# Small tensors behind the large ones in SBUF, convolved rows on a 64-byte step, and the sum of squares of the first half earlier at one of the layer boundaries

## The reference, cut to what matters

```
def rms_norm(x, g, eps):
    y = x * rsqrt(mean(x * x, axis=-1) + eps)
    return y * g

def causal_dwconv(x, w):          # out[t] = sum_j w[j] * x[t - 2 + j]
    ...

def hybrid_mixer(h, ...):
    proj = h @ w_in               # q, k, v of 2 dilated and 4 differential head pairs, 3 gated-conv groups
    ...                           # rotary, two kinds of attention, gated short convolution
    return concatenate([o_a, o_b, o_c]) @ w_out

def conv_glu_ffn(h, w_up, conv_w, w_down):
    g, u = split(h @ w_up)        # 22 tiles of 128 features
    g = causal_dwconv(g, conv_w)
    return (silu(g) * u) @ w_down

for layer in range(2):
    h = h + hybrid_mixer(rms_norm(h, norm_mix_g[layer]), ...)
    h = h + conv_glu_ffn(rms_norm(h, norm_ffn_g[layer]), ...)
return rms_norm(h, final_g)
```

## Time and profile before

| | |
|---|---|
| median of 3 runs | 2671.3 us |
| the profiled execution's own time | 2670.58 us |
| its span | 2668.6 us |
| mean granted PE clock | 0.969 of full |
| PE busy | 2489.0 us (93%) |
| DVE, POOL, ACT busy | 1525.8, 1189.1, 883.2 us |
| DMA | 130.28 MB, mean 49 GB/s |

### The profile page before, as it was taken

The page is one execution under the profiler, slowest core; times in us unless marked ns, Lnnn a source line. Parts: engine busy times, 40 slices in busy tenths (PEclk is TensorE's granted clock), DMA queues, the critical chain, the costliest instruction groups (busy, mean ns, idle before and its releaser), DMA issues.

```text
span 2668.6 us, 30947 instructions
## 1 busy us (share of the span) xinstructions
PE 2489.0 (93%) x11478; PEld 2014.4 (75%) x11478; DVE 1525.8 (57%) x2177; ACT 883.2 (33%) x1667; POOL 1189.1 (45%) x766
## 2 busy tenths in 40 slices
PE   8799999896999999999979999979879999999996
PEld 6688877774788888888768888768658888788884
DVE  8544677538555555555664456773575555555545
ACT  3344444313323232322414344442233232222322
POOL 3111122246666666665421112131576666566563
PEclk9899999897999999999989999989899999999998
DMA  3000011210111111111310010111101111111111
GB/s 138 24 25 25 31 32 43 80 56 16 48 51 60 48 48 48 64 51 60 109 46 25 24 32 25 32 62 44 48 32 48 48 64 52 59 48 48 48 48 63
DMA packets 53637, 130.28 MB, mean 49 GB/s; under 512 B 4720, under 2 KB 22256, under 8 KB 53488
## 3 DMA queue, kind: packets, MB, share of 16 engines
q1 hardware_dynamic: 51904, 127.03, 14.4%
q10 hardware_dynamic: 1584, 1.28, 0.2%
HBM read 118.59 MB, written 9.44 MB: 48 GB/s over the span
## 4 chain that ended last, share of the span: by engine, by line
PE 77%; DVE 12%; POOL 5%; issue 2%; ACT 2%; DMA 0%; POOLq 0%; DVEq 0%; SPq 0%; ACTq 0%
PE ps L744 16%; PE ps L745 16%; PE ps L746 16%; PE ps L711 6%; PE ps L713 6%; PE ps L712 6%; PE ps L938 3%; PE ps L925 2%; DVE h L1406 2%; POOL w_hi L544 2%; PE ps L912 1%; PE ps L913 1%; ACT prob L1168 1%; POOL w_lo L552 1%; DVE h L1404 1%
## 5 line engine op out<-in xcount | busy, mean ns | idle before, releaser
L518 POOL CAST w_hi<-stage 128x1024 fp32r<-128x1024 f32 (+1 forms) x66 | 67.7, 1026 | 860.1 <-PE ps L713 798.1
L711 PE MATMUL ps<-x_hi,w_hi 128*128 128x512 f32 x960 | 396.4, 413 | 9.1 <-issue 6.0
L552 POOL TENSOR_TENSOR w_lo<-more_stage,w_hi 128x512 fp32r<-128x512 f32 x202 | 289.3, 1432 | 225.1 <-ACT w_hi L1237 209.0
L713 PE MATMUL ps<-x_hi,w_lo 128*128 128x512 f32 x960 | 382.2, 398 | 0.0
L712 PE MATMUL ps<-x_lo,w_hi 128*128 128x512 f32 x960 | 382.0, 398 | 0.0
L552 POOL TENSOR_TENSOR w_lo<-stage,w_hi 128x512 fp32r<-128x512 f32 x194 | 276.8, 1427 | 229.1 <-ACT w_hi L1237 213.9
L1343 DVE TENSOR_TENSOR h<-ps,h 128x1024 f32<-128x1024 f32 x160 | 195.9, 1225 | 199.2 <-PE ps L746 196.2
L744 PE MATMUL ps<-T_hi,w_hi 128*128 128x512 f32 x704 | 285.1, 405 | 24.0 <-POOLq L555 8.8
L744 PE MATMUL ps<-mix,w_hi 128*128 128x512 f32 x704 | 281.3, 400 | 5.5 <-POOLq L555 5.5
L745 PE MATMUL ps<-T_lo,w_hi 128*128 128x512 f32 x704 | 282.1, 401 | 0.0
L746 PE MATMUL ps<-T_hi,w_lo 128*128 128x512 f32 x704 | 282.0, 401 | 0.0
(11 more groups left out here) (197 smaller groups left out, 4593.8 us busy)
## 6 DMA issues: line engine op xcount, KB each, us to landing
stage<-stream SPq DMA_DIRECT2D x112, 512.0 KB, 3.6
more_stage<-stream SPq DMA_DIRECT2D x68, 512.0 KB, 4.3
h<-x_t SPq DMA_DIRECT2D x16, 512.0 KB, 6.3
stage<-stream SPq DMA_DIRECT2D x16, 448.0 KB, 4.5
saved_h<-h SPq DMA_DIRECT2D x8, 512.0 KB, 4.8
h<-saved_h SPq DMA_DIRECT2D x8, 512.0 KB, 3.3
out_t<-h SPq DMA_DIRECT2D x16, 256.0 KB, 2.1
stage<-stream SPq DMA_DIRECT2D x16, 64.0 KB, 4.8
```

Of the source, the lines that this page charges most:

```text
L518: pool.tensor_copy(w_hi[:, s, wide], stage[:, s, wide]).then_inc(pool_seq, 1)
L552: pool.tensor_tensor(block_of(w_lo, n), raw, block_of(w_hi, n).bitcast(f32), ALU.subtract)\
L711: pe.matmul(out, w_hi[:, s, w], hi, start=start, stop=False)
L713: return pe.matmul(out, w_lo[:, s, w], hi, start=False, stop=stop)
```

## The change

Two things are changed.

The first is the layout. `padded`, `eye`, `ones`, `vec`, `gain` and six more small tensors are declared behind `more_stage`, the last of the large ones, with `eye` and `ones` ahead of `padded`. The zeros ahead of the convolved row become 16 (64 bytes) in place of 2; all slices of `padded` that began at TAPS - 1 begin at PAD. Starts in bytes beyond a multiple of 64, from the sizes of the tensors:

| | before | after |
|---|---|---|
| `h`, `stage`, `w_hi`, `w_lo`, `q_next`, `k_next` | 0 | 0 |
| `x_hi`, `x_lo`, `q_split`, `k_twice`, `k_lo`, `mix`, `prob`, `v_next`, `T`/`B` blocks, `more_stage` | 32 | 0 |
| centre of `padded` (read at L1227, used at L938, L1127, L1676) | 8 | 0 |
| `padded` one back, two back (L1704) | 4, 0 | 60, 56 |
| `eye`, `ones`, `vec` | 32 | 0 |

The second is the order of PE in `start_normed` where `fed` is not None, that is once in the program, between the feed-forward of layer 0 and the attention of layer 1.

```diff
+PAD = 16
...
-        padded = sbuf("padded", [P, TAPS - 1 + SEQ])
-        eye, ones = sbuf("eye", [P, P]), sbuf("ones", [P, P])
-        vec = sbuf("vec", [P, DEPTH, NV])
...
         more_stage = sbuf("more_stage", [P, F_SLOTS - W_SLOTS, D_MODEL])
+
+        eye, ones = sbuf("eye", [P, P]), sbuf("ones", [P, P])
+        padded = sbuf("padded", [P, PAD + SEQ])
+        vec = sbuf("vec", [P, DEPTH, NV])
...
                 heads_of_x(0, 1)
+                if fed is not None:
+                    sum_squares(0)
                 rests_of_x(0, 1)
                 heads_of_x(1, 1)
-                sum_squares(0)
+                if fed is not None:
+                    spread(0)
+                else:
+                    sum_squares(0)
                 rests_of_x(1, 1)
                 n = next_tile()
-                project_half(n, 0, THIRD[0], {3: lambda: spread(0), 6: lambda: sum_squares(1)})
+                if fed is not None:
+                    project_half(n, 0, THIRD[0], {6: lambda: sum_squares(1)})
+                else:
+                    project_half(n, 0, THIRD[0], {3: lambda: spread(0), 6: lambda: sum_squares(1)})
...
-                    dve.scalar_tensor_tensor(k_next[:, :], padded[:, TAPS - 1 - back:TAPS - 1 - back + SEQ], tap,
+                    dve.scalar_tensor_tensor(k_next[:, :], padded[:, PAD - back:PAD - back + SEQ], tap,
...
-            dve.memset(padded[:, 0:TAPS - 1], 0.0).then_inc(dve_seq, 1)
+            dve.memset(padded[:, 0:PAD], 0.0).then_inc(dve_seq, 1)
```

More of the change, by code:

```diff
@@ L252, in build @@
         more_stage = sbuf("more_stage", [P, F_SLOTS - W_SLOTS, D_MODEL])
+        eye, ones = sbuf("eye", [P, P]), sbuf("ones", [P, P])
+        padded = sbuf("padded", [P, PAD + SEQ])
+        vec = sbuf("vec", [P, DEPTH, NV])
+        gain = sbuf("gain", [P, KT])
+        neg_top = sbuf("neg_top", [P, 2, 2])
+        total_share = sbuf("total_share", [P, 2, 2, 2])
+        total, share = total_share[:, 0, :, :], total_share[:, 1, :, :]
+        head_sums = sbuf("head_sums", [P, 2, QB])
+        factor = sbuf("factor", [P, 2])
+        rs = sbuf("rs", [P, 3, QB])
         ps = ctx.enter_context(nc.psum_tensor("ps", [P, 8, HALF], f32))
@@ L267, in build @@
         squares = ((q_next[:, :], k_next[:, :], v_next[:, :], v_cur[:, :, :].rearrange("p b d -> p (b d)"),
-                    padded[:, TAPS - 1:], prob[:, 0, 1, :], prob[:, 1, 0, :], prob[:, 1, 1, :]),
+                    padded[:, PAD:], prob[:, 0, 1, :], prob[:, 1, 0, :], prob[:, 1, 1, :]),
                    (q_next[:, :], k_next[:, :], heads[:, :, :].rearrange("p b d -> p (b d)"), rstd_all[:, :],
-                    cos_t[:, :], sin_t[:, :], padded[:, TAPS - 1:]))
+                    cos_t[:, :], sin_t[:, :], padded[:, PAD:]))
         final_heads = v_next[:, :].rearrange("p (b d) -> p b d", d=P)
         diagonal = squares[0][0]
-        turned_groups = (padded[:, TAPS - 1:TAPS - 1 + HALF], padded[:, TAPS - 1 + HALF:])
+        turned_groups = (padded[:, PAD:PAD + HALF], padded[:, PAD + HALF:])
         low, high = slice(0, HEAD_DIM), slice(HEAD_DIM, P)
@@ L1089, in keep_first @@
                 act.wait_ge(product_done, PRODUCTS * (layer * F_TILES + f) + 1)
-                out = q_next[:, 0:HALF] if f else padded[:, TAPS - 1:TAPS - 1 + HALF]
+                out = q_next[:, 0:HALF] if f else padded[:, PAD:PAD + HALF]
                 act.activation(out, bank(STEADY[0][2]), ACT.Copy).then_inc(first_kept, 1)
@@ L1226, in conv_center @@
                 act.wait_ge(gate_ready, seen(gate_ready))
-                act.activation(out, padded[:, TAPS - 1:], ACT.Copy, scale=tap).then_inc(gate_used, 1)
+                act.activation(out, padded[:, PAD:], ACT.Copy, scale=tap).then_inc(gate_used, 1)
             def round_blocks(count):
@@ L1628, in first_blocks @@
                     rest("B21", k)
-                add_product(layer, 0, 2, padded[:, TAPS - 1:TAPS - 1 + HALF], 1, q_next[:, 0:HALF], first_kept)
+                add_product(layer, 0, 2, padded[:, PAD:PAD + HALF], 1, q_next[:, 0:HALF], first_kept)
                 dve.wait_ge(spread_done, 2 * norm + 2)
@@ L1649, in first_blocks @@
                     form("T4", k, "T2", "B21", ALU.subtract)
-                gates = padded[:, TAPS - 1:]
+                gates = padded[:, PAD:]
                 u2 = u3 = gates[:, 0:HALF]
@@ L1679, in combine @@
             def combine(layer, f):
-                gates, ups = padded[:, TAPS - 1:], q_next[:, :]
+                gates, ups = padded[:, PAD:], q_next[:, :]
                 low_gates, high_gates, low_ups, high_ups = gates[:, 0:HALF], gates[:, HALF:], ups[:, 0:HALF], ups[:, HALF:]
```

## The result

The changed kernel takes 2633.08 us (median of 4 runs, 2631.03 to 2633.65) against 2672.45 for the kernel before in the same series (4 runs, 2667.46 to 2674.71): ratio 0.9854, 95% interval 0.9837 to 0.9871. That is 39.4 us faster; 4.8 were predicted and 2655 was the low end of the range. The profiled execution took 2631.03 us, its span is 2629.2. What follows shows that the order gave some 3 to 7 us, about as predicted, and the layout about 35, where the prediction had put 0.

A forecast was written before the change was run, and what follows sets the result against it. PE, busy 93% of the span, was taken as the bound. The order's 3.15 + 1.65 = 4.8 us, with 0 for the layout, took 2671.3 to 2666.5, stated as 2666 us; range 2655 to 2673.

The forecast's parts named there:

- The order's term: Boundary into layer 1: PE's 3.15 us wait ahead of sum_squares(1) goes, with 1.65 us of low clock behind: 4.8 us.
- The steps: Boundary chain: sum_squares(0) without wait, roots(0) sooner, partial(1) ready before PE needs it, first scores 4.8 us sooner.
- One step: Boundary: with one POOL collision counted, DVE has partial(1) ready 2.4 us before PE arrives, so PE doesn't wait.
- Rival 1: Boundary gain doesn't reach the end: POOL and DVE meet otherwise or clock falls elsewhere; 2669 to 2673 us, chance 0.15.
- DVE, ACT and POOL: Layout on these engines: new row starts worth 0, though POOL's final-norm sum with `padded` goes from 1089 to 1290 ns.
- the cover named: Final norm: POOL's last sum ends 3.3 us before DVE asks for it, against 0.4 us of slowing.
- PE's moving side, taken as 0: Three-pass matmuls: moving rows going from 32 to 0 bytes were expected to change the spacing of 233.3 ns by nothing.
- The bounds, 3.3 ns either way: Phase effect per matmul, from wide scores at 230 ns against 233.3: -29 to +29 us over 8,880 matmuls.
- Rival 2: Three-pass matmuls: PE's moving reads get faster when rows start at 64 bytes; 2637 to 2658 us, chance 0.12.
- rival 3: Three-pass matmuls get slower because weights and moving rows now start at equal phases; 2695 us, chance 0.05.
- a nanosecond is worth 8.9 us: Each nanosecond saved on each of about 8,880 three-pass matmuls shortens the kernel by 8.9 us.

The follow-up runs named there:

- e1: The kernel before with only PE's new order at the boundary into layer 1, old layout kept: 2664.99 us, ratio to before 0.9978.
- e7: The changed kernel with 2 zeros instead of 16 ahead of the convolved row, its centre at 8 bytes again: 2630.48 us, ratio to before 0.9843.
- e3: The changed kernel with a 32-byte tensor ahead of everything large, so weights and moving rows all start at 32: 2630.14 us, ratio to before 0.9846.
- e4: The changed kernel with weights `w_hi` and `w_lo` at 32 bytes and moving rows at 0 of 64: 2666.75 us, ratio to before 0.9982.
- e8: The changed kernel with DVE's product of gate and value put behind its first down-projection add in ten pairs per layer: 2620.23 us, ratio to before 0.9803.

## Why the prediction was wrong

- **The order's term was right.** 4.8 us were predicted from two rows. The stretch to the first scores went from 65.2 to 60.4 us in the changed kernel, and by 4.3 us in e1, where no matmul is faster. e1 is the fair test; that the changed kernel shows 4.8 to the digit is in part luck, since the layout bears on that stretch too (65.8 us with the layout alone). The steps held: sum_squares(0) right behind heads(0,1) with no wait, DVE's idle time 2.61 us where 2.9 was said, an add of partial(1) colliding with POOL once more for 2.76 us, a clock of 1.00 behind, and 11.39 us ahead of the scores. One step was off by a little: partial(1)'s last three adds take 4.94 us, where partial(0)'s take 2.14, as the next L523 of POOL at 1336.35 meets one of them, so PE still waits 0.59 us where the prediction said none. It counted one collision, and there are two. Rival 1 (the gain doesn't reach the end) is refuted by e1, whose interval leaves 3.5 us or more.
- **DVE, ACT and POOL were right.** L1715 has 1283 ns at its least, as L1704 had; ACT's busy time is 882.2 us against 883.2; POOL's sum with `padded` rose from 1089 to 1264 ns where 1290 was said, under the cover named; in e7 the row's step makes no difference that the times show.
- **The step that failed: PE's moving side, taken as 0.** The sentence was "I take 0, since blocks that lie tens of kilobytes apart all show the one rate". They all lay at one phase, 32 against the weights' 0, so their one rate said nothing on what a phase does. The bounds, 3.3 ns either way, came from scores, which were no bound either: the scores' weights and rows share a phase in both kernels and their intervals didn't move (314, 235, 233, 236, 224, 231, 236 ns in both, for a row of them near 140 us), but they have their own rhythm and don't show the 226.7 of the three-pass matmuls. The term measured -6.67 ns, about 59 us over 8,880 matmuls before anything hides it.
- **Rival 2 named the place and not the mechanism.** Its time, 2637 to 2658, was the nearest. But "faster at 64 bytes" is not what happens: with all at 32 (e3) it is as fast, with the weights at 32 (e4) as slow as before. The one who looked at weights and moving rows together was rival 3, with the sign turned: equal phases don't get in each other's way, unequal ones do. The row it was weighed against, the scores with both at 32, could have been read for the other side.
- **Where the rest of 59 us went.** 34.6 came out (39.4 less 4.8). 12.9 are the difference between after and e8 (10 if e3 and e7 are taken for after): the faster PE runs into DVE's first add in the ten down projections of each layer. That wait was in no rival. The prediction wrote that a nanosecond is worth 8.9 us, which takes for granted that DVE's 43% of free time lies where it is needed; at that place it had 0.13 us. Of the other 12, 3 are that layer 1's feed-forward stretch is 14.3 us shorter in e8 where layer 0's is 17.7. About 7 are in the attention stages: from the first scores to the next first mix both layers together start 3,192 three-pass matmuls, which by 6.67 ns is 21 us, and got 14 us shorter. There the projections fell to 228.0 ns on average and not to 226.7, about 4 us, and PE's idle time stayed, 115 us before and 116 after. What sets both wasn't taken apart.

On ports the Trainium skill ("SBUF — State Buffer", section "Who interferes with whom") lists two independent SBUF read ports for PE, one for the moving operand and one for the weights. The runs don't agree with independence in the sense that neither slows the other: the rate of one stream depends on where the other's rows start (e3 against e4, 226.8 against 233.3 ns). By that, the layout would change nothing on PE; the measurement decides.

The rate that the Trainium skill gives for warm matmuls ("TensorE: Matmul & The Clock Gate", section "Wait — 56ns, not 53.3ns?"), 215.7 ns at 512 columns, is not reached at any phase tried here; 226.7 is the least.

What stays open: how the price comes about. 0, 64, 16, 32 and 4 bytes give 226.7, 229.0, 231.5, 233.3 and 236.7 ns. The order of the prices follows neither the distance nor any rule that was tried. That weights being loaded beside the running matmul and the moving rows meet in the memory is a guess that fits a cost of their relative start; no run here shows it.

## What to carry to other kernels

When PE is the bound, put the rows of weights and of moving operands at the same phase, counted modulo 128 bytes (both at 0 and both at 32 were equally fast here), and check it in the addresses, since one odd-sized small tensor allocated ahead of the large ones shifts everything behind it. A rate that is the same over all of a kernel is no evidence that nothing changes it: ask what all the cases have in common. And when PE gets faster throughout, look for the engine that was just in time before: here a fifth to a quarter of what the layout could give was lost to it (10 to 13 us beside 35) until one DVE step changed places.

## What the runs showed of the hardware

- With weights and moving rows of 4-byte elements, back-to-back 128x128 by 128x512 matmuls start every 226.7 ns when both start at the same phase (0 and 0, or 32 and 32), and every 233.3 ns when 32 bytes apart, in either direction. With moving rows 64, 16 and 4 bytes beyond the weights, one run each, it was 229.0, 231.5 and 236.7 ns: 4 bytes apart cost the most.
- POOL's sum of two 128x512 rows takes 1089 to 1092 ns with `padded` at 8 bytes of 64 and 1264 ns with it at 0 (final norm, before and e7 against after). The start off the 64-byte step was the faster one. DVE's shortest two-input pass over 1024 columns was 1283 ns with the row at 4 and 0 bytes of 64 and with it at 60 and 56.
